# A two-layer trunk on one core: reordering four turns of its attentions

## The reference

```python
for layer in range(2):
    hn = rmsnorm(x, g[0])
    mix = window_sink_attention(hn) if layer == 0 else topk_attention(hn)   # 16 query heads, 4 key heads, dim 64
    x = x + rmsnorm(mix, g[1])
    hn = rmsnorm(x, g[2])
    x = x + rmsnorm(square(relu(hn @ w_up)) @ w_down, g[3])
# topk_attention: score = sum_h relu(qi_h @ ki) * wi_h, causal; keep the top 128; softmax over the kept keys
```

## Time and profile before

| | |
|---|---|
| median of 3 runs | 1077.97 us (1077.39 to 1078.35) |
| profiled execution | 1077.35 us, of which the span of instructions is 1075.5 us |
| TensorE busy | 1055.0 us, 98% of the span |
| VectorE, ScalarE, GpSimd busy | 70%, 50%, 18% |
| first attention | about 50 to 155 us |
| second attention | about 603 to 715 us |
| granted TensorE clock, mean | 0.999 |

### The profile page before, as it was taken

The page is one execution under the profiler, slowest core; times in us unless marked ns, Lnnn a source line. Parts: engine busy times, 40 slices in busy tenths (PEclk is TensorE's granted clock), DMA queues, the critical chain, the costliest instruction groups (busy, mean ns, idle before and its releaser), DMA issues.

```text
span 1075.5 us, 14866 instructions
## 1 busy us (share of the span) xinstructions
PE 1055.0 (98%) x5408; PEld 857.9 (80%) x5408; DVE 747.9 (70%) x1284; ACT 538.1 (50%) x1016; POOL 192.8 (18%) x335
## 2 busy tenths in 40 slices
PE   9999999999999999999999989999999999999997
PEld 8777779888888888888778766679888888888885
DVE  5455536586697696687579898536596696696684
ACT  6677545353453443425554567745254444453432
POOL 0465320000000000005403387520000000000005
PEclk9999999999999999999999999999999999999999
DMA  9531505644545445432613333006553535535502
GB/s 298 118 79 41 118 1 119 135 93 104 107 90 118 99 97 118 91 66 52 136 41 79 79 79 80 1 1 145 111 113 84 118 82 115 117 79 118 112 7 78
DMA packets 52009, 99.94 MB, mean 93 GB/s; under 512 B 4704, under 2 KB 4832, under 8 KB 51936
## 3 DMA queue, kind: packets, MB, share of 16 engines
q1 hardware_dynamic: 51216, 98.61, 41.0%
q10 hardware_dynamic: 720, 0.38, 0.1%
HBM read 96.88 MB, written 2.10 MB: 92 GB/s over the span
## 4 chain that ended last, share of the span: by engine, by line
PE 86%; DVE 7%; DMA 3%; ACT 1%; issue 1%; POOL 1%; SPq 1%; POOLq 0%; DVEq 0%; ACTq 0%
PE bank L2048 11%; PE bank L2049 11%; PE bank L2050 11%; PE bank L2413 7%; PE bank L2414 7%; PE bank L2415 7%; PE bank L2058 6%; PE bank L2060 5%; PE bank L2059 5%; PE bank L2439 3%; PE bank L2437 3%; PE bank L2203 3%; PE bank L2438 3%; PE bank L2272 2%; DMA w_raw<-in_a_w_in 2%; PE bank L2258 2%
## 5 line engine op out<-in xcount | busy, mean ns | idle before, releaser
L2048 PE MATMUL bank<-r_hi,w_hi 128*128 128x512 f32 (+1 forms) x456 | 177.5, 389 | 0.0
L2049 PE MATMUL bank<-r_hi,w_lo 128*128 128x512 f32 (+1 forms) x456 | 177.4, 389 | 0.0
L2050 PE MATMUL bank<-r_lo,w_hi 128*128 128x512 f32 (+1 forms) x456 | 177.4, 389 | 0.0
L1645 DVE TENSOR_TENSOR w_lo<-w_raw,w_hi 128x1024 fp32r<-128x1024 f32 x84 | 102.1, 1223 | 70.5 <-ACT w_hi L1174 70.4
L1174 ACT ACTIVATE w_hi<-w_raw 128x1024 fp32r<-128x1024 f32 x84 | 87.8, 1055 | 119.1 <-PE bank L2050 82.9
L2413 PE MATMUL bank<-w_hi,hid_hi 128*128 128x512 f32 x336 | 130.7, 389 | 0.0
L2414 PE MATMUL bank<-w_lo,hid_hi 128*128 128x512 f32 x336 | 130.7, 389 | 0.0
L2415 PE MATMUL bank<-w_hi,hid_lo 128*128 128x512 f32 x336 | 130.7, 389 | 0.0
L819 POOL TENSOR_TENSOR acc<-acc,G 128x512 f32<-128x512 f32 x8 | 13.0, 1652 | 594.3 <-ACT waste L1033 594.3
L1183 ACT ACTIVATE w_hi<-w_raw,gT 128x512 fp32r<-128x512 f32 x96 | 64.6, 716 | 107.0 <-DMA w_raw<-in_w_mlp_up 75.5
L2050 PEld LDWEIGHTS bank<-r_lo,w_hi 128*128 128x128 f32 (+1 forms) x456 | 85.2, 187 | 18.3
(11 more groups left out here) (213 smaller groups left out, 2148.7 us busy)
## 6 DMA issues: line engine op xcount, KB each, us to landing
w_raw<-in_w_mlp_up SPq DMA_DIRECT2D x64, 512.0 KB, 6.5
w_raw<-in_w_mlp_down SPq DMA_DIRECT2D x64, 512.0 KB, 6.9
w_raw<-in_b_w_in SPq DMA_DIRECT2D x16, 512.0 KB, 6.8
w_raw<-in_a_w_in SPq DMA_DIRECT2D x8, 512.0 KB, 8.9
w_raw<-in_a_w_out SPq DMA_DIRECT2D x8, 512.0 KB, 5.8
w_raw<-in_b_w_out SPq DMA_DIRECT2D x8, 512.0 KB, 6.1
xt<-in_x_turned SPq DMA_DIRECT2D x8, 256.0 KB, 5.2
X<-in_x SPq DMA_DIRECT2D x4, 512.0 KB, 11.2
```

Source lines behind the costliest of these rows:

```text
L1645: nc.vector.tensor_tensor(half_of(w_lo[:, u % 2, :], a), b_of(PRODUCTS[i][1], a), half_of(w_hi[:, u % 2, :], a).bitcast(f32), ALU.subtract ...
L2048: nc.tensor.matmul(bank, whi, xhi, start=start, stop=False)
L2049: nc.tensor.matmul(bank, wlo, xhi, start=False, stop=False)
L2050: return nc.tensor.matmul(bank, whi, xlo, start=False, stop=stop)
```

## The change

Five edits.

1. First attention, turn 8 (`TURNED_WITHIN`): TensorE does half of the fill step, then turns the queries, then does the other half. ScalarE makes the high part of these queries after the exponentials of turn 9, and VectorE their low part after the reciprocal of turn 9.
2. First attention, turn 10: the same interruption, of the first of two fill steps; the other engines' order stays.
3. First attention, turn 11: the low part of unit 9 (`LAST_OUT`) is made in two instructions instead of one, with a semaphore after the first, right behind the masks; fill step 15 waits for the first before its first half and for the whole before its second.
4. Second attention: on VectorE `o_low` comes ahead of its half of unit 61 (turn 5); GpSimd makes the high part of unit 61 in turn 5 as before, but its low parts in turn 6, behind that turn's probabilities.
5. Second attention: `ROUNDS_2` has one more 11 at its front, so each of the last five rounds of block 2, and its mask, comes one turn later.

```diff
+TURNED_WITHIN = ((8, 10), ())
+
+LAST_OUT = 9
...
-            def shared_split():
-
-                w_h, w_l = w_place(SHARED)
-                whole = raw(RAW[SHARED][0])
+            def shared_high():
+
+                w_h, whole = w_place(SHARED)[0], raw(RAW[SHARED][0])
                 pool.wait_ge(*loaded(SHARED))
                 pool.wait_ge(*w_spent(w_before(SHARED)))
                 nc.gpsimd.tensor_copy(w_h[:, 1024:2048], whole[:, 1024:2048]).then_inc(shared_hi, 1)
+
+            def shared_low():
+
+                w_h, w_l = w_place(SHARED)
+                whole = raw(RAW[SHARED][0])
                 pool.wait_ge(shared_hi, 1)
...
                     for u in SPLITS[layer].get(n - 2, ()):
-                        if u in POOL_UNITS and u != SHARED:
+                        if u == SHARED:
+                            shared_low()
+                        elif u in POOL_UNITS:
                             split_low(u, (2, 3))
                     for u in SPLITS[layer].get(n - 1, ()):
                         if u == SHARED:
-                            shared_split()
+                            shared_high()
...
-                    for c, j in Q_TURN[layer].get(n, ()) if n >= 0 else ():
+                    inner = not layer and n == TURNED_WITHIN[0][0]
+                    for c, j in Q_TURN[layer].get(n, ()) if n >= 0 and not inner else ():
                         q_high(layer, q_no(layer, c, j))
...
                         expo(layer, n + 1, 3)
+                    for c, j in Q_TURN[layer].get(n, ()) if inner else ():
+                        q_high(layer, q_no(layer, c, j))
...
+                if u == LAST_OUT:
+                    nc.vector.tensor_tensor(w_l[:, 0:1024], whole[:, 0:1024], w_h[:, 0:1024].bitcast(f32), ALU.subtract).then_inc(last_out_lo, 1)
+                    last = nc.vector.tensor_tensor(w_l[:, 1024:2048], whole[:, 1024:2048], w_h[:, 1024:2048].bitcast(f32), ALU.subtract)
...
+                    if not layer and LAST_OUT in SPLITS[0].get(n - 1, ()):
+                        split(LAST_OUT)
...
+                    inner = not layer and n == TURNED_WITHIN[0][0]
+                    if inner:
+                        inverse(layer, n + 1)
...
                     if layer and n + 1 < TURNS:
                         inverse(layer, n + 1)
+                    if layer and n >= 3 and n % 2:
+                        o_low(layer, (n - 3) // 2)
...
-                    if n >= 3 and n % 2:
+                    if not layer and n >= 3 and n % 2:
                         o_low(layer, (n - 3) // 2)
...
-            ROUNDS_2 = (11, 12, 13, 14, 15, TOPK // 8)
+            ROUNDS_2 = (11, 11, 12, 13, 14, 15, TOPK // 8)
...
+                    if j == 0 and u == LAST_OUT:
+                        pe.wait_ge(last_out_lo, 1)
+                        dense(u, h, layer, d_no(layer, "out", c, j), q_reg(layer), j, (0, 1))
+                        ks = (2, 3)
...
-                    turned(n)
                     steps = FILL[layer].get(n, ())
+                    if n in TURNED_WITHIN[layer]:
+                        fill(steps[0], (0, 1))
+                        turned(n)
+                        fill(steps[0], (2, 3))
+                        steps = steps[1:]
+                    else:
+                        turned(n)
```

More of the change, by code:

```diff
@@ L362, in hybrid_trunk @@
         out_lo_done, shared_hi, shared_lo = sem("out_lo_done"), sem("shared_hi"), sem("shared_lo")
+        last_out_lo = sem("last_out_lo")
         setup_v, setup_g, trig_v, trig = sem("setup_v"), sem("setup_g"), sem("trig_v"), sem("trig")
@@ L1407, in split @@
                     return
-                if name[:3] == "out" or name[:3] == "mlp" and mlp_role(layer, u)[0] == "down":
+                if u == LAST_OUT:
+                    nc.vector.tensor_tensor(w_l[:, 0:1024], whole[:, 0:1024], w_h[:, 0:1024].bitcast(f32), ALU.subtract).then_inc(last_out_lo, 1)
+                    last = nc.vector.tensor_tensor(w_l[:, 1024:2048], whole[:, 1024:2048], w_h[:, 1024:2048].bitcast(f32), ALU.subtract)
+                elif name[:3] == "out" or name[:3] == "mlp" and mlp_role(layer, u)[0] == "down":
                     last = nc.vector.tensor_tensor(w_l, whole, w_h.bitcast(f32), ALU.subtract)
@@ L1541, in attention @@
                         inverse(layer, n + 1)
+                    if layer and n >= 3 and n % 2:
+                        o_low(layer, (n - 3) // 2)
                     for u in SPLITS[layer].get(n - 1, ()) if n > 0 else ():
-                        if u in NEXT_SLOT:
+                        if u in NEXT_SLOT and u != LAST_OUT:
                             split(u)
@@ L1546, in attention @@
                         split(4)
-                    if not layer and n + 1 < TURNS:
+                    if not layer and n + 1 < TURNS and not inner:
                         inverse(layer, n + 1)
-                    if n >= 3 and n % 2:
+                    if not layer and n >= 3 and n % 2:
                         o_low(layer, (n - 3) // 2)
```

## The result

The changed kernel takes 1079.39 us (median of 13 runs, 1077.94 to 1082.27), the kernel before 1077.71 us (13 runs beside it). The ratio is 1.0016, 95% interval 1.0009 to 1.0024: 0.16% slower. The forecast was 1077.6 us and a range up to 1079.2; the time lies 0.2 us above it. The profiled execution took 1079.05 us, with a span of 1077.3 us against 1075.5.

What follows compares the result with a forecast made beforehand. TensorE, working 98% of the span, bounds the kernel; a chain of waits over unit 63's load decides the second attention. Terms -1.4 + 1.0 = -0.4 us against the median of 1077.97 gave 1077.6 us, range 1073.4 to 1079.2.

Steps and rivals of the forecast that it cites:

- From there on all is as before: Second attention, behind the turn 9 scores: nothing further changes, so the delay there stays at +1.0 us.
- the forecast -0.4 us: Sum over both attentions: -1.4 us from the first, +1.0 us from the second.
- The second attention's mechanism: Unit 61's low parts end late, delaying unit 63's load and the turn 9 scores: +1.0 us, waits of 5.2 us.
- Rival B: Load of unit 63 does not hold TensorE back; the second attention keeps 3.2 us: 1073.4 us, chance 0.26.
- Rival C: Second attention: no lockout on GpSimd, -1.4 - 0.2, 1076.4 us, chance 0.14.
- Turn 11: First attention: fill step 15's whole wait for the low half of unit 9 goes, -1.10 us.
- Turns 8 and 10: First attention: turn 8's query wait goes, -0.56 us; turn 10 worth nothing since `o_low` holds step 12; together -0.43 us.
- the sum of -1.4: First attention in all: -0.43 - 1.10 + 0.1 us, the +0.1 for two extra interruptions of a fill step.
- The sign: Whole kernel, told apart beyond 0.2%: faster 0.28, same 0.62, slower 0.10.
- rival D: Second attention, turns 5 and 6: every VectorE instruction locks out GpSimd, unit 61 4.0 us late: 1080.6 us, chance 0.10.

Runs made afterwards that it cites:

- e3: Changed kernel with 12 extra repeated matmuls (same result) in TensorE's long wait before the turn 9 scores of the second attention: 1077.45 us, 0.9988 against the kernel before.
- e1: Changed kernel with GpSimd's low parts of unit 61 back in turn 5, ahead of the probabilities of turn 6: 1075.83 us, 0.9973 against the kernel before.
- e10: e1 with unit 9's low part made in one instruction behind the gain multiplication, as before the change: 1077.15 us, 0.9986 against the kernel before.
- e2: Kernel before with only the edits of the first attention: 1076.8 us, 0.9985 against the kernel before.
- e6: e1 with block 2's rounds in their old turns: 1077.33 us, 0.9995 against the kernel before.
- e5: e1 with the old order of turns 8 and 10 of the first attention, no interrupted fill step: 1075.96 us, 0.9983 against the kernel before.
- e9: e1 with ScalarE's and VectorE's old order in turn 8 of the first attention, TensorE's fill step still interrupted: 1076.16 us, 0.9975 against the kernel before.
- e8: Changed kernel with 6 extra repeated matmuls in the long wait before the turn 9 scores: 1079.43 us, 1.0010 against the kernel before.
- e4: Kernel before with only the edits of the second attention: 1081.32 us, 1.0021 against the kernel before.

## Why the prediction failed, step by step

- **The step that failed is "From there on all is as before".** I had forecast one TensorE wait of 4 us or more and charged it with its idle time alone. Its other price, the clock at half behind it, is in no term and no bound: 1.52 us in the profiled execution, where the other places come to the forecast -0.4 us. e3 fills the wait and changes nothing else that the trace shows, and its 0.9988 is at or under the forecast (0.9996).
- **The second attention's mechanism was right.** The chain of waits held in each link: probabilities first, both engines taking turns, low parts late, load, ScalarE, VectorE, scores. I gave +1.0 us, the traces have +1.06. The waits at and before the scores were forecast as 5.2 us, 4 or more in one; they are 5.5 us, but the longest is 3.43. Rival B is out by e1: a load issued 2.2 us earlier brings the scores 2.1 us earlier. Rival C is out too (GpSimd's four probability instructions took 3.31 us in the changed kernel instead of 2.34, as VectorE's half of 1.28 us fell among them; I had let it fall on the low parts).
- **Turn 11: right place, wrong size.** -1.10 forecast, -1.49 in the trace. I took the idle time of the row, 1.10; e10 shows that the wait costs 1.44.
- **Turns 8 and 10: half right.** I said turn 10 would bring nothing because `o_low` of pair 3 holds the step. It did: the step waited 0.83 us. (The profile names the split `L1426`, but `o_low`, at 106.00 to 106.66, ends just ahead of the step at 106.76.) For turn 8 I kept 0.56 and, after turn 10, 0.43. It was +0.02. What I had wrong is the cover of the queries' low half: I compared it with the scores only. It also frees the bank that the second set of transposes needs. That wait shows as 0.15 us, but from the transposes to the scores it is 1.33 us (99.59 to 100.92) instead of 0.96, and the masks of turn 10 and `o_low` behind them come 0.4 us later than I had reckoned.
- **Luck in the first attention.** Two errors of 0.4 to 0.5 us with opposite signs, at turns 8 and 11, made the sum of -1.4 come out at -1.47. That it fits is luck.
- **The sign.** I gave "slower" 0.10, by a rival in which GpSimd is locked out by every VectorE instruction. It was slower by another way: the waits came together behind the late load, and the clock fell there, where no wait of size is left to pay for it. Of rival D nothing is seen.

## What to carry to other kernels

Follow the chain of waits before moving work: an instruction that releases a load belongs ahead of one whose result is only wanted later, even if both seem equally near. When a removed wait reappears further on, do not book it at its idle time alone: behind it TensorE can run at half its clock, and here even useless matmuls in the gap paid. Ask too what lies behind a wait, since a later wait can pay for such a fall, and behind the last long one nothing does. Price a removed wait by the distance between two same instructions with and without it, not by the idle time shown.

## What the runs showed of the hardware

The clock did not fall by the wait's length alone. It fell behind waits of 1.69 us (e2, e6), 2.50 us (e5, e10) and 3.43 us (the changed kernel), and stayed at 1.00 behind 1.69 and 1.98 us (before), 2.50 us (e1), 2.52 us (e9), 2.20 us (e8) and 3.34 us (e4). The same instructions with the same wait did both, so it is a matter of the execution too.

What a fall costs depends on what follows. It was 1.52 us in the changed kernel, behind its last long wait. It was 0.69 us in e5 and 0.38 us in e10 (531.56 against e1's 531.18), where the clock was at half for as long, 3.4 us, but the 0.82 us wait before the turn 9 scores was still to come and vanished.

The kernel before is not free of it. Its trace has a mean clock of 0.999, which only 9 of its 83 executions beside the experiments reach; their mean is 0.996, as that of the changed kernel. So the prediction read a trace without a fall, the ratios hold the falls of both kernels, and this may be why e3 gains more by its ratio (1.3 us) than by its distances; that is argued, not shown. By the traces, what the change did was to put a fall where it counts in full. Whether more than one wait of an execution can be hit, no profile here shows.
